# Two transformer blocks on one core: weight slabs stored in their on-chip layout, squares added by VectorE, modulation chunks and mixing steps in other places of the schedule

## The reference, cut to what matters

```python
mod = silu(c) @ w_ada + b_ada                 # six vectors of 1024: sh1 sc1 g1 sh2 sc2 g2
h = rmsnorm(x, norm1_g) * (1 + sc1) + sh1
proj = h @ w_in                               # q (8 heads of 64), k, v (2 heads), u_pool (4 groups of 128)
q, k = rope(rmsnorm(q)), rope(rmsnorm(k))
att = softmax(q k^T / 8) v                    # grouped heads, no mask
pool = (windowed mean(u_pool) - u_pool) @ w_pool * pool_scale
x = x + g1 * (concat(att, pool) @ w_out)
h2 = rmsnorm(x, norm2_g) * (1 + sc2) + sh2
x = x + g2 * conv_gated_ffn(h2, w_up, conv_w, conv_b, w_down)
# second block: own w_ada_2, indexed sparse attention, stick-breaking attention, gates, w_out_2, w_ff1_2, w_ff2_2
```

## Time and profile before

| | us |
|---|---|
| median of 3 runs | 1480.93 |
| lowest, highest | 1478.17, 1481.79 |
| profiled execution, its own time | 1484.66 |
| its span, first to last instruction | 1482.50 |
| TensorE busy in the span | 1389.2 (94%), mean granted clock 0.961 |
| VectorE, ScalarE, GpSimd busy | 814.7, 648.2, 710.4 |

### The profile page before, as it was taken

One profiled execution on the slowest core, in us unless ns is written; L12 is line 12 of the kernel. 1 busy time (PEld: TensorE's weight loads), 2 busy tenths in 40 slices (PEclk: granted clock), 3 DMA queues, 4 the chain that ended last, 5 costly groups with the idle time before them and its releaser, 6 DMA issues.

```text
span 1482.5 us, 17943 instructions
## 1 busy us (share of the span) xinstructions
PE 1389.2 (94%) x7087; PEld 1161.3 (78%) x7087; DVE 814.7 (55%) x1372; ACT 648.2 (44%) x1203; POOL 710.4 (48%) x389
## 2 busy tenths in 40 slices
PE   5958886899999999998999999999999999999998
PEld 5746675888888888896787777878898888888886
DVE  6765544566767666465678886552438431212224
ACT  4533552444333242363477774455455432323231
POOL 3343733265656456455243355336834663645660
PEclk6869898899999999998999999999999999999999
DMA  9542225155555555323213222113331223232221
GB/s 301 180 149 58 71 72 170 58 179 203 186 199 199 182 192 172 121 86 86 57 58 85 58 57 58 57 57 114 100 100 32 83 85 114 85 111 88 89 109 57
DMA packets 134227, 167.56 MB, mean 113 GB/s; under 512 B 14208, under 2 KB 109312, under 8 KB 134144
## 3 DMA queue, kind: packets, MB, share of 16 engines
q1 hardware_dynamic: 134144, 166.42, 34.8%
HBM read 164.31 MB, written 2.10 MB: 112 GB/s over the span
## 4 chain that ended last, share of the span: by engine, by line
PE 80%; DVE 8%; ACT 5%; DMA 3%; POOL 2%; issue 1%; SPq 0%; DVEq 0%; ACTq 0%
PE B L543 77%; DMA ZF<-in_w_ada 1%; DVE ZF L1851 1%; ACT WH L1169 1%; PE B L947 1%; PE B L769 1%; POOL WL L2307 1%; DMA RAW<-in_w_in 1%; DVE G L1851 1%; DVE SC L2158 1%; DVE ZF L2133 1%; ACT SC L1330 1%; ACT ZR L1320 1%; DMA RAW<-in_w_up 0%; DVE M L2131 0%
## 5 line engine op out<-in xcount | busy, mean ns | idle before, releaser
L2307 POOL TENSOR_TENSOR WL<-RAW,WH 128x512 fp32r<-128x512 f32 (+2 forms) x202 | 468.5, 2333 | 485.7 <-ACT WH L1169 440.9
L543 PE MATMUL B<-HH,WH 128*128 128x512 f32 (+2 forms) x1024 | 400.5, 394 | 10.8 <-ACT G L1347 4.3
L543 PE MATMUL B<-HH,WL 128*128 128x512 f32 (+2 forms) x1024 | 394.2, 387 | 0.0
L543 PE MATMUL B<-HL,WH 128*128 128x512 f32 (+2 forms) x1024 | 382.6, 386 | 8.6 <-DVE HL L1783 8.6
L1169 ACT ACTIVATE WH<-RAW 128x512 fp32r<-128x512 f32 (+2 forms) x202 | 190.4, 975 | 203.0 <-PE B L543 178.3
L543 PEld LDWEIGHTS B<-HH,WH 128*128 128x128 f32 x1024 | 195.6, 191 | 52.4 <-ACT G L1347 5.1
L543 PEld LDWEIGHTS B<-HH,WL 128*128 128x128 f32 x1024 | 195.5, 191 | 38.6
L543 PEld LDWEIGHTS B<-HL,WH 128*128 128x128 f32 x1024 | 190.1, 190 | 45.0 <-DVE HL L1783 10.8
L543 PE MATMUL B<-ZR 128*128 128x256 f32 (+4 forms) x1048 | 157.3, 339 | 31.7 <-ACT SC L1330 10.7
L543 PEld LDWEIGHTS B<-ZR 128*128 128x128 f32 (+1 forms) x1048 | 124.9, 199 | 61.1 <-issue 17.4
L543 PE MATMUL B<-ZR,WH 128*128 128x512 f32 (+1 forms) x624 | 164.8, 352 | 0.7 <-POOL WL L2307 0.7
(11 more groups left out here) (241 smaller groups left out, 1759.0 us busy)
## 6 DMA issues: line engine op xcount, KB each, us to landing
ZF<-in_w_ada SPq DMA_DIRECT2D x86, 512.0 KB, 4.4
RAW<-in_w_ff SPq DMA_DIRECT2D x32, 1024.0 KB, 5.3
RAW<-in_w_up SPq DMA_DIRECT2D x22, 1024.0 KB, 5.1
RAW<-in_w_in SPq DMA_DIRECT2D x16, 1024.0 KB, 5.2
RAW<-in_w_in SPq DMA_DIRECT2D x19, 512.0 KB, 5.2
RAW<-in_w_down SPq DMA_DIRECT2D x8, 1024.0 KB, 5.1
G<-in_w_ada SPq DMA_DIRECT2D x10, 512.0 KB, 6.5
RAW<-in_w_out SPq DMA_DIRECT2D x4, 1024.0 KB, 5.2
```

Source lines behind the costliest of these rows:

```text
L543: return e.matmul(out, l, r, start=start, stop=stop)
L2307: e.tensor_tensor(lo[:, at], k.RAW[:, i % 2, at], hi[:, at].bitcast(F32), ALU.subtract).then_inc(*w.hit((i, q)))
```

## The change

- **Slabs.** The host writes every slab into one array `slabs` of [number, 128 partitions, 2048], each partition's row as it lies on chip. SP loads a slab with a single DMA whose rows are up to 8 KB. x is stored by partition too, so that its four loads have rows of 4 KB.
- **Squares.** VectorE adds the squares of tiles 1 to 7 to tile 0's as they come; TensorE sums only the result (4 matmuls in place of 32, each of them two records). `row(0)` and `row(1)`, the copies of the two rows of silu(c), are moved: row(0) after the first add, row(1) after the Newton steps.
- **ScalarE's order** of slab quarters against `rounded` tiles in stage 2: slab 0's first two quarters behind the wide inverse root, the others behind tile 0's rounding; tile 6 between the halves of q23, the fill of V's zeros last.
- **Modulation chunks.** The four points "0" are gone; the attention has a chunk at every odd step from 1 to 31, sixteen in all.
- **Attention schedule.** p0 goes into the loop: p0, p1, p2, p3 begin at steps 1, 6, 11, 16, in a ring of two banks in place of one; the pool products come at 21 to 27; splits at 0, 12, 21; the first halves of the mixing tiles at 29, 31, 33, 34.
- **SP's order.** Slabs are issued at steps 0, 4, 8, 18, 27, and slabs 9 and 10 right behind the attention's chunks, ahead of those of the points "2".

```diff
-T1 = {"p0": -4, "p1": 5, "p2": 9, "p3": 13}
-POOL_OUT = {19: 0, 21: 1, 23: 2, 25: 3}
-SPLIT1 = {t + q: q for t in (0, 14, 28) for q in range(4)}
+T1 = {"p0": 1, "p1": 6, "p2": 11, "p3": 16}
+POOL_OUT = {21: 0, 23: 1, 25: 2, 27: 3}
+MIX = {29: 0, 31: 1, 33: 2, 34: 3}
+SPLIT1 = {t + q: q for t in (0, 12, 21) for q in range(4)}
...
+def packed(a):
+    table = slabs()
+    out = np.zeros((len(table), 128, 2048), np.float32)
+    for i, (nk, nn, pick) in enumerate(table.values()):
+        out[i, :, 0:nk * nn] = pick(a).reshape(128, nk * nn)
+    return out
...
-        many = {"0": 2, "1": p in range(9, 33, 3), "2": 2, "gate": 2, "val": 2, "down": 2 - point[1]}[g]
+        many = {"1": p in range(1, 33, 2), "2": 2, "gate": 2, "val": 2, "down": 2 - point[1]}[g]
...
 (pe_program)
-    for m in range(8):
-        pe.wait_ge(sq[0, m])
-        for q in range(4):
-            t = mm(b[:, q:q + 1], k.squares[m][:, 128 * q:128 * q + 128], ONES[:, 0:1], m == q == 0, m == 7 and q == 3)
+    pe.wait_ge(acc[0, 7])
+    for q in range(4):
+        t = mm(b[:, q:q + 1], k.squares[0][:, 128 * q:128 * q + 128], ONES[:, 0:1], q == 0, q == 3)
...
-    proj("p0", "p01", 0, hx, ring="p")
-    B.deal(main=(0,), a=(1,), s=(2, 5, 3), t=(6, 7), o=(4,))
+    B.deal(main=(1, 0), s=(2, 5, 3), t=(6, 7), o=(4,))
...
-        if 32 <= s < 36:
-            mix(s - 32, 0, 4, ("main", "a", "s", "s")[s - 32])
+        if s in MIX:
+            mix(MIX[s], 0, 4, ("main", "main", "s", "s")[MIX[s]])
...
 (act_program)
-    quarters(0, 1)
     act.wait_ge(v_root["y", 0])
...
-    quarters(1, 4)
+    quarters(0, 2)
     rounded(0)
+    quarters(2, 4)
     rounded(1)
...
     rounded(5)
-    quarters()
+    quarters(0, 2)
+    rounded(6)
+    quarters(2, 4)
+    rounded(7)
     act.wait_ge(k.sig("in_cst")[0])
...
 (dve_program)
+    def squares(*ms):
+        for m in ms:
+            dve.wait_ge(a_sq[0, m])
+            if m > 1:
+                dve.wait_ge(acc[0, m - 1])
+            e.tensor_tensor(k.squares[0], k.squares[0], k.squares[m], ALU.add).then_inc(*acc.hit((0, m)))
+    wide(0)
+    wide(1)
+    squares(1)
+    row(0)
+    squares(2, 3, 4, 5, 6, 7)
...
-    ada_point(("0", 0))
     head_scaled("q0")
     head_scaled("k")
-    ada_point(("0", 1))
     rotated("q0", *QKS["q0"][:2])
     rotated("k", *QKS["k"][:2])
-    ada_point(("0", 2))
     head_newton("q1")
-    ada_point(("0", 3))
...
 (sp_program)
-            nk, nn, segs = k.slabs[k.names[i]]
             if i > 1:
                 sp.wait_ge(w_lo[i - 2, 3])
-            for dst, src in segs(k.raw(i)):
-                load(f"in_w{i % 2}", i, dst, src)
+            n = k.size(i)
+            load(f"in_w{i % 2}", i, k.RAW[:, i % 2, 0:n], a["slabs"][i, :, 0:n])
...
-    for p in range(4):
-        for n in k.chunks["0", p]:
-            ada(n + 2)
     for s in range(STEPS1):
-        if s in (0, 4, 12, 20, 30):
+        if s in (0, 4, 8, 18, 27):
             weights()
...
+    weights()
+    weights()
     for m in range(4):
         for n in k.chunks["2", m]:
             ada(n + 2)
     for i in range(5, len(k.names)):
-        if i > 6:
+        if i > 8:
             weights()
```

56 lines of the change are left out of this document (24 added, 32 removed).

## The result

| | before | changed |
|---|---|---|
| median, us | 1481.36 (4 runs) | 1459.87 (4 runs) |
| lowest to highest | 1478.17 to 1484.14 | 1457.09 to 1465.07 |
| profiled execution, its own time | 1484.66 | 1457.09 |
| its span | 1482.50 | 1455.3 |
| TensorE / VectorE busy | 1389.2 / 814.7 | 1370.3 / 826.9 |

The ratio is 0.986 with an interval of 0.9825 to 0.9894: the change makes the kernel 21 us faster, where 34 had been forecast. The same kernel timed again beside other experiments gave 1460.26 (1457.64 to 1463.23, 4 runs), ratio 0.9858 (0.9827 to 0.989).

A forecast was written before the change was run, and what follows sets the result against it. TensorE fills the last 1217.85 us; only the first 264.65 can move, paced partly by VectorE. Terms -13.5, -14.5, -3.3, -2.6 sum to -33.9: from 1484.66 to 1450.8, or 1447.0 as a median (3.73 lower); range 1434 to 1464.

The forecast's parts named there:

- Parts 1 to 3: Everything up to the attention's first scores: these start at 77.0 instead of 90.47 us, -13.5 together.
- Part 4: Attention, 16 units: waits go, p0 and sums come in; 95 instead of 109.55 us, -14.5.
- Part 5: Unit 15 to the first output tile: the first mixing half moves ahead, another fills a wait; -3.3 us.
- Part 6: Second norm, from the first residual: a stall of 10.61 us goes, a new one of 9 comes; -2.6.
- the rest: The last stage, 1217.85 us with TensorE busy for 1196.09, matmuls untouched: carried over as it is.
- Part 1: Sum of squares at the start: VectorE's adds bring the logarithm to 15.2 and unit(0) to 18.5 us; -2.8.
- Part 2: Single slab loads, h's projections: TensorE's wait after late slab q23 goes; -1.3 us, total -4.1 at their end.
- Part 3: Ahead of the attention: eight sums and p0 leave, first scores at 77.0 us; -13.5 with the earlier 4.1 included.
- Rival 1: The attention doesn't shrink: p0 and eight sums fill the waits that go; 1461.5 us, chance 0.20.
- rival 3: Slower: every attention sum takes 2.33 us on the chain beside GpSimd; +16.6, 1497.5 us, chance 0.05.

The follow-up runs named there:

- f1_again: The changed kernel run once more, unaltered; median 1460.3 us, ratio 0.986 to the kernel before.
- g1: The changed kernel with TensorE summing all squares again and slabs loaded in several pieces from the original arrays; median 1468.4 us, ratio 0.989 to the kernel before.
- f2: The changed kernel with eight of the attention's sixteen sums moved back to four points ahead of it; median 1465.4 us, ratio 0.989 to the kernel before.
- e1: The changed kernel with slab 10 issued behind the eight chunks of the output GEMM; median 1455.2 us, ratio 0.982 to the kernel before.

## Why the prediction was right in sign and too large

Terms in us against before; the last column from the profile of the changed kernel.

| step | predicted | measured |
|---|---|---|
| Parts 1 to 3, first scores | -13.5 | -12.3 |
| Part 4, units 0 to 15 | -14.5 | -7.5 |
| Part 5, to R0 | -3.3 | -2.8 (-1.2 in f1_again) |
| Part 6, R0 to norm | -2.6 | +0.2 |
| the rest | 0 | -4.7 |

The span fell by 27.2 in this pair of profiles; the medians, which average over clock patterns, by 21.5.

**Part 1** held: 15.47 against 15.2, unit(0) at 18.50. Its size depends on the clock that the old series met, 2.8 against the profile of before and 5.8 in g1; the prediction took the one profile for the rule. **Part 2** failed in its step "That wait goes: -1.3": a wait of 4.39 became 2.61, h's projections ended at 58.5 instead of the forecast 57.6, 43.0 after the logarithm where before had 43.5, and without the single load it is 43.1 (g1). TensorE's wait for ScalarE went, and one for VectorE's low part came. That 0.5 is within the 1.0 between the two profiles of the changed kernel. **Part 3** held with 78.1 against 77.0; f2 shows that the sums and the slab behind their loads were the reason.

**Part 4** is the term that was mis-sized. The mechanism was named (a sum stands "after the low part of the unit before and ahead of the next unit's maxima"), but then priced at "0 to 1 each" for the units after 10 and at nothing by itself in the walk up to unit 10. The conclusion "Units of 6.3 on average hide it mostly" was drawn from the mean load of VectorE in units 10 to 15, where four sums stood in five units. What the runs showed: 9.3 us for the sums, none of it in units 6 to 13, where "hide it mostly" was right, even in units as short as 4.7. In units 0 to 6, 5.8: VectorE has the head work of q1 to q3 there as well, and three sums of 2.23 stand on the chain. In units 13 to 15, 3.5: the chain runs through GpSimd, and the sums make it slower. So the order in VectorE's queue and the two lengths of a sum were read rightly, but they were priced by the mean load of a stretch and not at the units in which a sum stands on the chain. Without the sums the attention takes 92.7, two less than the 95 forecast for it with them. Rival 1's time, 1461.5, is the nearest to what came, and that is luck: it kept the attention at 110, which became 102, and the rest of the distance lies in Part 6.

On how VectorE and GpSimd disturb each other: the Trainium skill, "SBUF — State Buffer", section "SBUF: two separate sides", has the two engines shut each other out for a whole instruction. The rows agree in kind: sums of 2.3 beside sums of 1.28, and GpSimd's two groups 10 and 20% shorter once the sums are gone. But not each sum that meets GpSimd is a long one, as the prediction took it to follow: the sum at 162.60 takes 1.27, and the low part that GpSimd began 0.15 later, at 162.75, takes 2.25 instead of some 1.25, while at 99.35 the sum began behind GpSimd's rotation step and took 2.31. One of the two pays, and the three sums on the chain were of the kind that pay. The mean sum is 1.65, and rival 3, which priced every one at 2.33 and whole on the path, would have had the attention some 25 us longer for the sums alone. It was 7.5 shorter.

**Part 5** held: -2.8 and -1.2 in two profiles of the same kernel, a spread that lies in the clock (1.00 and 0.94).

**Part 6** had the right wait and the wrong sum. SP at +8.5 (forecast +7.9), chunk 18 landed at +14.3 (+14), VectorE's wait 10.47 (9), residuals of tiles 2 and 3 at +17.4 and +23.1 (+17.8, +22.5): up to here all held. The fifth tile's residual came at +29.7, not +27.0, mostly because the last pair took 6.6 where 4.5 had been set: both loads were waited for (0.24 and 1.27), and the added squares took 1.75 beside GpSimd's low part of slab 9, where they take 0.69 alone. The square of the fifth tile was added at +30.6, exactly as before. The new stall ate the old one's gain, and e1 shows that it was a matter of one issue's place.

**The rest**, carried over as it is, was 4.7 shorter. That is hardly an effect of the change: all thirteen profiles of the changed kernel and its variants have 1212.5 to 1213.3 or 1214.8 to 1215.2 in it, also the one with the old loads and squares, and both values occur for the same kernel, 1213.1 and 1215.2. Where the two profiles of the changed kernel part (a hundred microseconds each, from 400 us after the norm's start, columns as in the earlier trace rows; the changed kernel first, then f1_again):

```profile
642.17:742.17 100.00, 93.64 (x496) 74.98 (x495) 65.39 (x128) 54.85 (x125) 42.23 (x28) 0.98 0.20 70
```

```profile
644.61:744.61 100.00, 93.86 (x482) 75.20 (x481) 63.60 (x122) 52.27 (x119) 42.71 (x29) 0.95 0.18 64
```

The same place in the program, clock 0.98 against 0.95, and 496 matmuls got through against 482. Before's single profile has 1217.9, with 0.95 there and 0.98 in a later stretch where the others have 1.00. Without the 4.7 the profiled pair differs by 22.5, near the medians' 21.5. Why the stage falls into one or the other is open, and so is whether before ever has the shorter one, since there is one profile of it.

## What to carry to other kernels

An engine that is 60 or 80% busy over a stage can still be the one that sets its pace: look at what its queue holds between two dependent instructions, not at the mean. Price a filler unit by unit: in full, at its long length, where that engine is on the chain (here three of sixteen, 2.2 us each), at nothing where another engine is (here seven), and where the chain runs through GpSimd, at what the filler takes from GpSimd. A mean price, 0.6 here, is right for none of them. Put fillers where the engine is idle in long pieces (here the output GEMM behind the last unit), and spread them so that their loads land between, and none stands ahead of the last product. In a load queue, an issue that waits for a buffer belongs behind the loads that are ready.

## What was not expected of the hardware

- The last stage takes 1213 or 1215 us for the same instructions, and the stretch behind unit 15 takes 26.15 or 27.7 with granted clock 1.00 or 0.94. The Trainium skill, "TensorE: Matmul & The Clock Gate", section "Part 1: The HAM clock gate (the "warmup" mystery)", says that the same kernel meets more or fewer slow matmuls from run to run; these rows agree, with 1.6 and 2 us for one stage of a profile.
- Work on VectorE slows GpSimd as well as the other way: 1326 to 1467 ns for a low part, 1605 to 2005 for a scaling, with 16 sums more in 100 us.
- 0.21 us a record for the small summing matmuls in g1, 0.14 in before. The clock row of g1's profile reads 1.00 from the start to 46 us, yet its 128x512 matmuls between 26 and 46 us start 0.43 apart, as they do in other profiles at 0.50, where at 1.00 it is 0.23. In that profile the row does not tell the speed there.
- 134227 DMA packets became 32196, and a slab's median time to landing went only from 5.1 to 5.3 down to 4.9 us; what the single load saves is SP's issue time, 0.43 for 5.88, and at the median 0.3 us (against before, 4.4) to 0.5 us (against g1, 4.7) on a chunk load of 512 KB beside it.
